# Retention's chunks in another order and in other banks, and the scan's B and C of the samples spread through memory

## The reference, cut to what matters

```python
def retention_chunk(state, q, k, v, log_gamma):      # 128 tokens, 4 heads, k 64 wide, v 128 wide
    ...
    scores = jnp.einsum('bthd,bshd->bhts', q, k) * decay[None]
    inner = jnp.einsum('bhts,bshe->bthe', scores, v)
    cross = jnp.einsum('bthd,bhde->bthe', q, state) * ...
    new_state = state * jnp.exp(l * log_gamma)[None, :, None, None] + jnp.einsum('bshd,bshe->bhde', kdec, v)
    return new_state, inner + cross
...
def ssd_chunk(state, x, dt, bm, cm, a):              # 8 groups; bm and cm are 128 wide for each
    ...
    y_off = jnp.einsum('btgn,bghpn->btghp', cm, state) * jnp.exp(acs)[..., None]
    new_state = state * jnp.exp(acs[:, -1])[..., None, None] + jnp.einsum('bsgn,bsgh,bsghp->bghpn', bm, dec_end, xdt)
    return new_state, y_diag + y_off
```

## Time and profile before

| | us |
|---|---|
| median of 3 runs | 3417.2 (3415.84 to 3420.82) |
| the profiled execution's own time | 3418.3 |
| its span in the profile | 3416.5 |
| TensorE busy | 3243.2 (95%) |
| VectorE, ScalarE, POOL busy | 1527.9, 1143.8, 1206.0 |
| granted clock of TensorE, mean | 0.968 |

### The profile page before, as it was taken

The page is one execution under the profiler, slowest core; times in us unless marked ns, Lnnn a source line. Parts: engine busy times, 40 slices in busy tenths (PEclk is TensorE's granted clock), DMA queues, the critical chain, the costliest instruction groups (busy, mean ns, idle before and its releaser), DMA issues. The chain is left out here.

```text
span 3416.5 us, 56741 instructions
## 1 busy us (share of the span) xinstructions
PE 3243.2 (95%) x20604; PEld 3060.4 (90%) x20604; DVE 1527.9 (45%) x2686; ACT 1143.8 (33%) x2132; POOL 1206.0 (35%) x889
## 2 busy tenths in 40 slices
PE   7889988988999999999999999999899999999998
PEld 6569984667999999999898989898889999999998
DVE  3699993523221212122557677767742212122122
ACT  3512214623321213132445555445532412122222
POOL 2206844312312222223365455566443221222222
PEclk9989999968999999999999999999999999999999
DMA  4218646022311111112222233221441111111111
GB/s 136 54 31 144 194 160 223 8 78 90 45 49 44 48 48 44 49 43 82 56 83 93 82 94 100 80 94 57 150 138 49 43 50 43 49 43 49 43 49 69
DMA packets 344008, 263.90 MB, mean 77 GB/s; under 512 B 52134, under 2 KB 308150, under 8 KB 341910
## 3 DMA queue, kind: packets, MB, share of 16 engines
q1 hardware_dynamic: 327926, 232.18, 22.7%
q0 software_dynamic: 8192, 19.13, 1.6%
q10 hardware_dynamic: 7776, 11.09, 1.5%
HBM read 219.43 MB, written 44.76 MB: 77 GB/s over the span
## 5 line engine op out<-in xcount | busy, mean ns | idle before, releaser
L234 POOL TENSOR_TENSOR w_low_sb<-w_loaded_sb,w_high_sb 128x1024 fp32r<-128x1024 f32 (+1 forms) x278 | 569.3, 2055 | 1550.9 <-ACT w_high_sb L226 1527.1
L252 PE MATMUL psum<-act_high_sb,w_high_sb 128*128 128x344 f32 (+1 forms) x2400 | 770.0, 321 | 10.6 <-PEq L985 5.7
L252 PE MATMUL psum<-act_low_sb,w_high_sb 128*128 128x344 f32 (+1 forms) x2400 | 768.3, 320 | 0.0
L252 PE MATMUL psum<-act_high_sb,w_low_sb 128*128 128x344 f32 (+1 forms) x2400 | 768.1, 320 | 0.0
L252 PE MATMUL psum<-second_high_sb,w_high_sb 128*128 128x344 f32 x1728 | 553.3, 320 | 0.5 <-PEq L2382 0.5
L252 PE MATMUL psum<-second_low_sb,w_high_sb 128*128 128x344 f32 x1728 | 551.9, 319 | 0.0
L252 PE MATMUL psum<-second_high_sb,w_low_sb 128*128 128x344 f32 x1728 | 551.9, 319 | 0.0
L252 PEld LDWEIGHTS psum<-act_high_sb,w_high_sb 128*128 128x128 f32 (+1 forms) x2400 | 451.1, 188 | 12.1 <-issue 10.8
L252 PEld LDWEIGHTS psum<-act_high_sb,w_low_sb 128*128 128x128 f32 (+1 forms) x2400 | 451.4, 188 | 0.4
L252 PEld LDWEIGHTS psum<-act_low_sb,w_high_sb 128*128 128x128 f32 (+1 forms) x2400 | 451.1, 188 | 0.4
L226 ACT CAST w_high_sb<-w_loaded_sb 128x1024 fp32r<-128x1024 f32 (+1 forms) x230 | 239.5, 1043 | 518.6 <-PE psum L252 498.0
(11 more groups left out here) (434 smaller groups left out, 4812.9 us busy)
## 6 DMA issues: line engine op xcount, KB each, us to landing
w_loaded_sb<-in_w_up SPq DMA_DIRECT2D x64, 512.0 KB, 4.0
w_loaded_sb<-in_w_down SPq DMA_DIRECT2D x64, 512.0 KB, 3.6
w_loaded_sb<-in_w_in_odd SPq DMA_DIRECT2D x48, 512.0 KB, 4.0
key_pages_sb<-in_cache_k SPq DMA_DIRECT2D x64, 256.0 KB, 3.1
ecay_sum_spread_sb<-decay_sum_scratch SPq DMA_DIRECT2D x8, 2048.0 KB, 9.8
w_loaded_sb<-in_w_in_even SPq DMA_DIRECT2D x28, 512.0 KB, 3.9
value_pages_sb<-in_cache_v SPq DMA_DIRECT2D x52, 256.0 KB, 4.9
gated_scratch<-gated_sb POOLq DMA_DIRECT2D x8, 1032.0 KB, 4.4
```

Of the source, the lines that this page charges most:

```text
L234: ins = self.nc.gpsimd.tensor_tensor(self.wl[:, par, k, 0:width], self.wf[:, par, k, 0:width], self.wh[:, par, k, 0:width].bitcast(F32), A ...
L252: ins = nc.tensor.matmul(out, w[:, par, k, 0:width], a[:, k, cols], start=n == 0, stop=n == 3 * KT - 1)
```

## The change

In retention:

- four pairs of banks in turn for the transposes, in place of two;
- the scores in banks 0 and 1 or 4 and 5, the chunk state in bank 6 or 7, the output always in 2 and 3;
- TensorE's order is chunk state n, scores n+1, output n; the output takes two heads' full products, then the same two heads' 64-row products;
- POOL scales q of all eight chunks at once (eight buffers), then spreads the samples' k (before on VectorE), then makes the low halves of the weights;
- the samples' update, products and waits are split in two halves of four samples.

In the scan the diagonals and their products go. SyncE stores B and C of the eight samples from `post` to a scratch tensor in HBM, turned, one element at a time, and loads B back to all partitions with a zero step; POOL issues the same load for C where it made the second diagonals. SyncE's queue now has the weights of unit 1 first, then a wait for the convolution's last output (`conv_out`), the two stores, the samples' states, the load of B, and the rest of the weights.

```diff
-    qdb = B.take("q_decayed_sb", [P, 2, 2, P])
+    qdb = B.take("q_decayed_sb", [P, NBLK, 2, P])
...
             for n in range(NBLK):
-                if n == 2:
-                    low_ahead(B, pool)
-                if n >= 2:
-                    pool.wait_ge(s_o, n - 1)
-                nc.gpsimd.tensor_tensor(qdb[:, n % 2], qk[:, 0:2, n * P:(n + 1) * P], qdecay, ALU.mult).then_inc(s_qd, 1)
+                nc.gpsimd.tensor_tensor(qdb[:, n], qk[:, 0:2, n * P:(n + 1) * P], qdecay, ALU.mult).then_inc(s_qd, 1)
+            pool.wait_ge(s_kept, NBLK + 2)
+            nc.gpsimd.tensor_tensor(kd, srow[:, 0:256].unsqueeze(1).to_broadcast([NS, NS, 256]),
+                                    B.ident[0:NS, 0:NS].unsqueeze(2).to_broadcast([NS, NS, 256]), ALU.mult).then_inc(s_kd2, 1)
+            low_ahead(B, pool)
...
                 dve.wait_ge(s_st, n + 1)
+                if n >= 1:
+                    dve.wait_ge(s_o, n)
...
-            dve.wait_ge(s_outer, 1)
-            for c in range(2):
...
+            for half in range(2):
+                dve.wait_ge(s_outer, half + 1)
+                b = slice(4 * half, 4 * half + 4)
+                for c in range(2):
...
-                if n >= 2:
-                    pe.wait_ge(s_kept, n - 1)
-                    pe.wait_ge(s_kd, n - 1)
+                if n >= 4:
+                    pe.wait_ge(s_kept, n - 3)
+                    pe.wait_ge(s_kd, n - 3)
...
+            def chunk_out(n):
+                pe.wait_ge(s_scd, n + 1)
                 if n >= 1:
+                    pe.wait_ge(s_okept, n)
+                out = lambda h: B.psum[:, 2 + h % 2, (h // 2) * P:(h // 2 + 1) * P]
+                if n >= 1:
+                    pe.wait_ge(s_qd, n + 1)
                     pe.wait_ge(s_state, 2 * n)
...
+                for c in range(HR // 2):
+                    for h in (2 * c, 2 * c + 1):
+                        ins = nc.tensor.matmul(out(h), vrow[:, n, h * P:(h + 1) * P], scd[:, n % 2, h, :], start=True, stop=n == 0)
+                    for h in (2 * c, 2 * c + 1) if n >= 1 else ():
+                        ins = nc.tensor.matmul(out(h), state[rows_of(h), (n - 1) % 2, h // 2, :], qdb[rows_of(h), n, h // 2, :],
                                                start=False, stop=True)
                 ins.then_inc(s_o, 1)
+
+            pe.wait_ge(s_kept, NBLK + 2)
+            pe.wait_ge(s_kd, NBLK)
+            scores(0)
+            for n in range(NBLK):
+                chunk_state(n)
+                if n + 1 < NBLK:
+                    scores(n + 1)
+                chunk_out(n)
...
+    def load_spread(eng, g, i):
+
+        eng.wait_ge(s_bcs, g * 32 + 32)
+        B.hold(eng)
+        eng.dma_start(spr[:].rearrange("p b n -> p (b n)"),
+                      bass.AP(tensor=B.bc_scratch.tensor, offset=g * (2 * NS * P) + i * NS * P,
+                              ap=[[0, P], [1, NS * P]])).then_inc(s_spr[i], 16)
...
+                    if nx is not None:
+                        load_unit(nx, 1)
+                    sp.wait_ge(S["conv_out"], g * 4 + 4)
+                    B.hold(sp)
+                    with nc.allow_non_contiguous_dma("B and C of eight samples, turned"):
+                        for i in range(2):
+                            sp.dma_start(B.bc_scratch[bass.ds(g, 1), i].rearrange("o b n -> n (o b)"),
+                                         post[:, 2 + i, SEQ:TOK]).then_inc(s_bcs, 16)
                     sp.wait_ge(s_sto, g * (16 * NS))
...
+                    load_spread(sp, g, 0)
                 if nx is not None:
-                    for e in range(1, 6):
+                    for e in range(1 if g is None else 2, 6):
                         load_unit(nx, e)
...
-                if g is not None:
-
-                    pool.wait_ge(S["conv_out"], g * 4 + 4)
-                    pool.wait_ge(S["sample_gated"], g)
-                    diagonals(2)
...
-                        diagonals(3)
+                        load_spread(pool, g, 1)
...
-            def spread(g, m):
-
-                await_group(pe, S["diagonal"], g, 2, m + 1)
-                if m == 0:
-                    pe.wait_ge(S["state_rows"], g)
-                    pe.wait_ge(S["sample_scaled"], g)
-                for a in range(2):
-                    ins = nc.tensor.matmul(B.psum[:, 6 + a, :], B.ones[:],
-                                           dg[:, 4 * a:4 * a + 4, :].rearrange("p b n -> p (b n)"), start=True, stop=True)
-                ins.then_inc(S["spread"], 1)
...
                 pe.wait_ge(S["sample_gated"], g + 1)
+                pe.wait_ge(S["sample_mean"], g)
...
-                    ins = nc.vector.tensor_tensor(tmp[:, c], B.psum[:, 6:8, :].rearrange("p a (b n) -> p (a b) n", b=4),
+                    ins = nc.vector.tensor_tensor(tmp[:, c], spr[:],
```

More of the change, by code:

```diff
@@ L2180, in scores @@
             def scores(n):
-                if n >= 1:
-                    pe.wait_ge(s_scd, n)
-                for h in range(HR):
-                    q = slice(64 * (h % 2), 64 * (h % 2) + 64)
-                    ins = nc.tensor.matmul(B.psum[:, h % 2, (h // 2) * P:(h // 2 + 1) * P], qk[q, 2 + h // 2, n * P:(n + 1) * P],
-                                           qk[q, h // 2, n * P:(n + 1) * P], start=True, stop=True)
-                ins.then_inc(s_sc, 1)
-            for n in range(NBLK):
-                scores(n)
+                if n >= 2:
+                    pe.wait_ge(s_scd, n - 1)
@@ new lines, in scores, with chunk_state @@
+                for h in range(HR):
+                    ins = nc.tensor.matmul(B.psum[:, 4 * (n % 2) + h % 2, h // 2 * P:(h // 2 + 1) * P], qk[rows_of(h), 2 + h // 2, n * P:(n + 1) * P],
+                                           qk[rows_of(h), h // 2, n * P:(n + 1) * P], start=True, stop=True)
+                ins.then_inc(s_sc, 1)
+            def chunk_state(n):
+                if n >= 2:
+                    pe.wait_ge(s_state, 2 * n - 2)
+                for h in range(HR):
+                    ins = nc.tensor.matmul(B.psum[rows_of(h), 6 + n % 2, h // 2 * P:(h // 2 + 1) * P],
+                                           kdec[:, n, h * DKR:(h + 1) * DKR], vrow[:, n, h * P:(h + 1) * P], start=True, stop=True)
+                ins.then_inc(s_st, 1)
@@ L2721, in mamba_groups @@
     early = B.top
-    dg = B.take("diagonals_sb", [P, NS, P])
+    spr = B.take("sample_b_or_c_sb", [P, NS, P])
     sml = B.take("sample_small_sb", [P, 8, 16])
@@ L3035, in slot @@
                     scan(g, k - 1)
-                if k == 2:
-                    spread(g, 0)
-                if k == 5:
-                    spread(g, 1)
                 if k == NBLK:
@@ L3081, in turn_state @@
                 await_group(pe, S["state"], g, NBLK, NBLK)
+                pe.wait_ge(S["state_rows"], g)
                 for j in range(2):
```

85 lines of the change are left out of this document (31 added, 54 removed).

## The result

The changed kernel takes 3474.2 us (median of 4 runs, 3470.9 to 3490.9), the kernel before 3418.3 beside it: ratio 1.0173, 95% interval 1.0140 to 1.0207. It is 56 us slower; 13 us faster was forecast. The profiled execution has a span of 3469.3 us.

A forecast was written before the change was run, and what follows sets the result against it. TensorE's own queue and its waits were taken as the bound. Retention -35, the scan's rounds +16 and its last group +6 sum to -13, from 3417.2 to 3404 us, with a range of 3368 to 3430.

The forecast's parts named there:

- 16 in the rounds: Scan: late states and a low clock, less the removed spread, cost +2.3 us a round, seven times +16.
- 6 in the last group: Scan's last group: gated tiles 13 us late, TensorE 9, some given back by later work and spreads: +6 us.
- Forecast -35: Retention: shorter chunks at full clock and no POOL wait start the next stage 35.5 us earlier, less 1: -35 us.
- Rival C: Retention: the clock stays at 1.2 GHz, so the whole change gives 0, 3417 us; chance 0.13.
- 13 us were taken for two: Scan, SyncE: the two element stores take 13 us, half of the 26 us measured for four similar stores.
- Rival A: Scan: the element stores land fast, in about 2 to 11 us; -48 in all, 3369 us; chance 0.30.
- 1 us for what is behind: Scan, SyncE: the sample states behind the stores need 1 us more, landing 14 us after the convolution.
- rival B: Scan: sample states land later behind the stores, deciding from 15.7 us after the convolution; +46, 3463 us; chance 0.15.
- 2.7 + 1.3, seven times: Scan rounds: late states delay the weight split and TensorE by 2.7 us; the low clock after it costs 1.3.
- Two replaced by the issue of one load (worth 0): Scan, POOL: two of its four removed 1 us products give way to issuing one load, worth 0.
- -1.7 a round: Scan, TensorE: removing the first spread is worth 0, the second, between tiles, gives 1.7 us a round.
- 1.3 us a round for the clock: Scan: after standing still over 5 us, TensorE's clock runs low and loses 1.3 us a round.

The follow-up runs named there:

- ret_alone: The kernel before with only the diff's retention part, the scan as before: 3381.8 us, ratio 0.9893.
- runs32: The changed kernel, with B and C of the samples stored as they lie, in 32-byte runs instead of turned single elements: 3419.0 us, ratio 1.0007.
- states_first: The changed kernel, with SyncE issuing the sample states' loads ahead of the two element stores again: 3438.6 us, ratio 1.0053.
- states_rows: The changed kernel with the states' loads ahead of the element stores and the conv rows where the gates come last: 3428.7 us, ratio 1.0028.
- filler4: states_rows plus four small unused POOL products between C's load and the adds of the samples' states: 3400.0 us, ratio 0.9944.
- kept_products: states_rows plus two pairs of unused TensorE products at the places of the removed spreads: 3424.1 us, ratio 1.0017.
- both_kept: states_rows with filler4's POOL products, kept_products' TensorE products and raw_first's order of the gated tiles' loads: 3390.0 us, ratio 0.9909.
- raw_first: states_rows, with the last group's gated tiles' loads issued ahead of SyncE's wait for the convolution and the element stores: 3421.3 us, ratio 1.0003.
- rows_apart: The changed kernel, with the conv rows in the last two chunks' gated rows and VectorE's wait moved to the seventh gate: 3482.1 us, ratio 1.0191.
- after_decay_later: The changed kernel, with POOL making the samples' decay after the low half of the weights: 3437.2 us, ratio 1.0052.
- c_later: states_rows, with POOL issuing C's load after the four adds of the samples' states instead of ahead of them: 3428.8 us, ratio 1.0024.

## Why the prediction was wrong

Retention came out as forecast. The scan was to cost 22 us (16 in the rounds, 6 in the last group) and costs 92 (ret_alone against the changed kernel).

**Retention: right.** Forecast -35, measured -36 (ret_alone). The chunk took 3.36 us (3.45 forecast), the samples' outer products 3.7 (3.6), the clock held 1.00 until 729 us, and POOL's wait was gone. One wait of 1.46 us for VectorE's first decays wasn't in the sum. Rival C is out. The edits next to each other there (pairing of shapes, no wait) were not separated.

**The stores: nearly right.** 13 us were taken for two; they took 12.0 to 14.7 in the seven rounds, and 10.6 to 11.5 with the states' loads out of the way. Rival A is out. runs32 shows that the count of pieces is the cause, as the earlier trace rows suggested. Its pieces of 32 bytes are under 512 bytes as well, so that limit, which the prediction named, doesn't tell the two cases apart.

**"1 us for what is behind": the first step that failed.** The states were to be there 14 us after the convolution, and their decay began 18.1 us after it. The 1 MB behind the stores doesn't follow them in 1 us: in the seven rounds the last state landed 16.4 to 17.8 us after the convolution, whether its eight issues took 4.7 us (first round) or 11.77 (fourth). That put the case beyond the 15.7 us from which rival B decides. Here the mechanism was right and the size was not: the sum had 28 us for it (2.7 + 1.3, seven times), and the order of the two is worth 35.5 (states_first). That rival B's price (+46) is nearest to what happened (+56) is in part luck: 28.7 and 9.9 us of the scan's loss came from two steps that B didn't have.

**A wait that wasn't in the sum.** The conv rows' stores, POOL's, meet the same transfers on their way, and VectorE's first gate needs their buffer: 3.2 us of TensorE in the fourth round, 1.8 to 3.2 in the seven. The Trainium skill ("DMA: Bandwidth & Descriptors", Issuing engines are not separate DMA queues) says that transfers of all issuing engines run on the same 16 DMA engines; the trace agrees (VectorE's wait for them fell from 5.0 to 1.7 us a round when only SyncE's order was changed). On top of the first it is worth 9.9 us (states_rows).

**"Two replaced by the issue of one load (worth 0)": the costliest step that failed.** The two products of POOL ahead of the adds were costed as work off the path. Without them POOL's adds meet VectorE's x_dt in another order, and that takes 5.74 us in place of 0.85. Worth: 28.7 us (filler4 against states_rows). The Trainium skill ("SBUF — State Buffer", Who interferes with whom) says that a VectorE instruction with two inputs in SBUF contends with a GpSimd instruction that reads SBUF, and calls the ports that they share an exclusive lock. The trace agrees that the two contend (both inputs of x_dt are in SBUF, and so are those of the adds), but one instruction of POOL is 1.28 us here, and the product stood through five of them, not one. By the same rule VectorE's outer product, whose spread input the change moves from PSUM to SBUF, becomes one that can contend: two of them took 3.77 us in most rounds (2.45 before), where the prediction put a fraction of a us. It isn't the place of the input by itself: in states_rows, with the same input, they took 2.45 in all seven rounds. Whether TensorE waited for them isn't shown.

**The removed spreads: -1.7 a round was wrong in sign or zero.** The first only lengthened a wait, as the text said; but in states_rows that wait, 2.7 to 3.1 us, came with a low clock in each round, and with the products (0.9 to 1.7 us) it didn't. The prediction took 1.3 us a round for the clock. In the changed kernel TensorE is busy for 677.1 us in the seven rounds and in ret_alone for 665.3, though 3.4 us of products a round are gone, so by an estimate from these the clock cost 5.1 us a round. kept_products and both_kept put the worth of the products' *staying* at 2.5 to 5 us in all, which is hardly more than the noise.

**The last group: +6 forecast, +17 measured** (tail of 1003 against 986 in ret_alone), of it 7.5 by the gated tiles' place (raw_first); the mechanism was right, the size not: the first tile's wait was 13.35 us, 9 were taken.

The sum of the scan, from ret_alone to the changed kernel:

| term | forecast us | measured us |
|---|---|---|
| order of states and stores, with the clock behind the wait | 28 | 35.5 |
| conv rows | none | 9.9 |
| POOL's 2 us of second diagonals | 0 | 28.7 |
| TensorE's removed products | -12 | 2.5 |
| last group (measured: the gated tiles' place alone) | 6 | 7.5 |
| stays in both_kept | none | 8.3 |
| sum | 22 | 92.4 |

Each is the step in this order of edits (the tiles' 7.5 were measured from states_rows, and the products' 2.5 are both_kept against filler4 less these); in another order the shares differ, since the waits cover one another (rows_apart alone: nothing).

**Open.** What lets POOL pass VectorE over isn't settled. The moment alone isn't it: x_dt was starved when it began 0.53 us into the first add (after_decay_later) and not when it began 0.70 us (kernel before) or 0.32 us (filler4) into it; in the last two POOL had made other products directly ahead. That alone doesn't decide it either: c_later has no such products, and its x_dt, begun 0.21 us into the third add, took 1.34 us. Nor is what the remaining 8.3 us are.

## What to carry to other kernels

Before a chain of products is replaced by a store and a load, count the pieces of the store, list everything that shares its queue or lands during it, the tiny stores of other engines too, and ask what stands behind each waiting instruction: a decay that nobody hurried for held up the weights. Removing work from an engine that isn't the bound was not free here, and need not be elsewhere: it moves that engine's long instructions against another's, and it can turn cover of TensorE into a wait. The cheapest cure was to let what is awaited first go first: one condition changed on POOL gave 13 us with the old scan, and 37 in the changed kernel.

## What the runs showed of the hardware that was not expected

- Two stores of 1,024 elements of 4 bytes took 10.6 to 11.5 us (states_first), and 12.0 to 14.7 with 1 MB of loads issued behind them; in runs of 32 bytes they landed after 1.4. Eight issues of 128 KB behind them took 4.7 to 11.8 us of SyncE in the changed kernel's rounds, 4.45 in the fourth round behind the runs of 32 bytes.
- A VectorE product of 128x256 from SBUF to SBUF, normally 0.42 us, took 5.74 to 7.27 us while POOL ran adds and splits (SBUF to SBUF too) without a pause; POOL's four adds took 4.99 us then, and 5.64 when VectorE's product came through in 1.23.
- In the fourth rounds of these kernels the granted clock was 0.50 for 3.4 to 13.7 us around or behind waits of TensorE of 2.7 us and more, though what follows is work without a gap; around those of 1.0 to 1.8 us it stayed at 1.00. It isn't a fixed rule: in filler4's second, fifth and seventh rounds it stayed at 1.00 behind waits of 2.75 us, and in the kernel before it fell for 3.4 us in the second and fifth rounds (from 1868 and 2168 us) with no wait above 1.04 us near.
